# Two transformer blocks in one kernel: the normalised activations are placed at other byte offsets

## The reference

```
a = rmsnorm(h, norm1); proj = a @ w_in            # pool input, q/k/v of two kinds of attention, forget gates
h = h + concat(pool, forgetting attention, stick-breaking attention) @ w_out
h = h + (silu(n @ w_gate) * (n @ w_up)) @ w_down   # n = rmsnorm(h, norm2), inner width 2816
x = rmsnorm(h, final_norm)[:, 16:]
```

```
x = x + 0.5 * rmsnorm(swiglu(rmsnorm(x), w_ffn1_in, w_ffn1_out))
x = x + rmsnorm(mixer(rmsnorm(x)))                 # a gated convolution and a two-directional mLSTM
x = x + 0.5 * rmsnorm(swiglu(rmsnorm(x), w_ffn2_in, w_ffn2_out))
```

## Time and profile before

| | |
|---|---|
| median of 3 executions | 793.31 us (793.28 to 793.38) |
| the profiled execution | 793.85 us, its span 792.0 us |
| instructions | 12209 |
| TensorE busy, weight loads busy | 781.6 us (99%), 687.9 us |
| VectorE, ScalarE, GpSimd busy | 533.2, 429.3, 28.3 us |
| matmuls | 4710 |
| read from HBM | 139.69 MB, 178 GB/s over the span |

### The profile page before, as it was taken

How to read it: one execution, slowest core, us unless ns; L and a number is a source line. 1 busy time by engine, 2 the same in 40 slices (tenths; PEclk the granted TensorE clock), 3 DMA queues, 4 the chain that set the end, 5 groups by cost and what they waited for, 6 DMA issues and landing times.

```text
span 792.0 us, 12209 instructions
## 1 busy us (share of the span) xinstructions
PE 781.6 (99%) x4710; PEld 687.9 (87%) x4710; DVE 533.2 (67%) x628; ACT 429.3 (54%) x565; POOL 28.3 (4%) x35
## 2 busy tenths in 40 slices
PE   9999999999999999999999999999999999999997
PEld 8989988888888888888888887999988888888885
DVE  7866657766666667866666566766977766666665
ACT  6556657544544448744544447565557654454444
POOL 0000000000000000000000000002520000000000
PEclk9999999999999999999999999999999999999999
DMA  9633433645555553665545554452444664555521
GB/s 335 235 110 112 143 115 128 245 166 205 191 183 209 175 196 110 238 224 199 198 176 209 183 188 159 142 204 108 161 165 162 221 223 166 205 192 183 208 106 54
DMA packets 20797, 141.16 MB, mean 178 GB/s; under 512 B 2448, under 2 KB 2704, under 8 KB 4384
## 3 DMA queue, kind: packets, MB, share of 16 engines
q1 hardware_dynamic: 20192, 138.65, 48.8%
q0 software_dynamic: 576, 2.10, 0.8%
HBM read 139.69 MB, written 1.05 MB: 178 GB/s over the span
## 4 chain that ended last, share of the span: by engine, by line
PE 94%; ACT 2%; DVE 2%; issue 1%; DMA 1%; SPq 0%; DVEq 0%; ACTq 0%
PE ps L1478 93%; ACT whi L695 1%; PE ps L1484 1%; DMA raw<-wstream 1%; DVE x L1227 0%; ACT squared L710 0%; DVE xa L1034 0%; PE ps L1707 0%; DVE wlo L1023 0%; PE ps L1677 0%; PE ps L1926 0%; DVE xg L1222 0%; DVEq L272 0%; ACT L928 0%; PE ps L1709 0%
## 5 line engine op out<-in xcount | busy, mean ns | idle before, releaser
L1478 PE MATMUL ps<-xa,whi 128*128 128x512 f32 (+2 forms) x1744 | 377.4, 347 | 0.0
L1023 DVE TENSOR_TENSOR wlo<-raw,whi 128x2048 fp32r<-128x2048 f32 x128 | 293.6, 2295 | 82.2 <-ACT whi L695 82.2
L1478 PEld LDWEIGHTS ps<-xa,whi 128*128 128x128 f32 x1744 | 299.6, 188 | 41.4 <-issue 2.1
L695 ACT ACTIVATE whi<-raw 128x2048 fp32r<-128x2048 f32 x128 | 244.2, 1909 | 6.9 <-PE ps L1478 6.8
L1478 PE MATMUL ps<-xa,wlo 128*128 128x256 f32 (+1 forms) x1376 | 219.8, 278 | 0.0
L1478 PEld LDWEIGHTS ps<-xa,wlo 128*128 128x128 f32 x1376 | 187.9, 188 | 2.8
L1478 PE MATMUL ps<-wlo,hhi 128*128 128x512 f32 x240 | 93.5, 390 | 0.0
L1478 PE MATMUL ps<-whi,hlo 128*128 128x512 f32 x240 | 93.5, 390 | 0.0
L1478 PE MATMUL ps<-whi,hhi 128*128 128x512 f32 x240 | 93.5, 390 | 0.0
L889 ACT ACTIVATE hhi<-arena 128x512 fp32r<-128x512 f32 x30 | 19.0, 633 | 88.4 <-PE ps L1478 81.9
L875 ACT ACTIVATE arena<-ps 128x512 f32<-128x512 f32 x33 | 19.7, 597 | 85.5 <-PE ps L1478 85.4
(11 more groups left out here) (221 smaller groups left out, 531.6 us busy)
## 6 DMA issues: line engine op xcount, KB each, us to landing
raw<-wstream SPq DMA_DIRECT2D x128, 1024.0 KB, 4.8
gain_row<-rows_in POOLq DMA_DIRECT2D x4, 512.0 KB, 3.9
x<-x_in SPq DMA_DIRECT2D x2, 512.0 KB, 4.0
raw<-wstream SPq DMA_DIRECT2D x2, 512.0 KB, 5.8
out<-x SPq DMA_DIRECT2D x4, 256.0 KB, 2.1
xg<-const_in SPq DMA_DIRECT2D x1, 912.0 KB, 11.8
small<-small_in SPq DMA_DIRECT2D x1, 152.0 KB, 6.1
arena<-meta_in SPq DMA_DIRECT2D x1, 64.0 KB, 4.5
```

What stands on the lines that cost most here:

```text
L695: nc.scalar.activation(whi[slot][:], raw[slot][:], ACT.Copy).then_inc(hi_ready, 1)
L1023: nc.vector.tensor_tensor(wlo[slot][:], raw[slot][:], whi[slot][:].bitcast(F32), ALU.subtract).then_inc(lo_ready, 1)
L1478: return nc.tensor.matmul(o, lhsT, rhs, start=start, stop=stop, skip_group_check=True)
```

## The change

The start of the view `xn[k]` moves. In bytes from the beginning of `xa` it was 320 for all four. Now it is 128 in the first FFN, 256 in the second, 448 in the mixer and 384 in the third FFN. Which half of a tile is high and which is low stays as it is (`XN_HI`). No instruction, wait or transfer is added or removed.

```diff
--- before.py
+++ after.py
@@ -46,7 +46,7 @@
 GROUPS = FF // 256
 UNIT = 2048
 SLOTS = 3
-XN_AT = ((80, SEQ),) * 4
+XN_AT = ((32, SEQ), (64, SEQ), (112, SEQ), (96, SEQ))
 XN_HI = (0, 0, 0, 0)
 EPS = 1e-6
 NEG = -1e30
```

## The result

The changed kernel takes 800.59 us (800.46 to 801.46, 3 runs) against 793.31: 1.009 of the time of before, 95% interval 1.0076 to 1.0104. It is slower by 7.3 us, where I had forecast slower by 2.9 and a range to 799.5. The profiled execution has a span of 798.6 us against 792.0, at a full clock again.

The account below looks back on a forecast made before the run. TensorE, busy 781.6 of 792.0 us, was taken to bound the kernel. Low products +3.8, second FFN's 512-column products -0.9 and mixer 0 gave +2.9 us: 796.2 us from a median of 793.31, range 790.0 to 799.5.

Parts of the forecast that it names:

- What bounds the kernel: Whole kernel: TensorE sets the end, so any change in the distance between two matmuls' starts arrives one for one.
- The low products lose the clean pace: FFN loops: 256-column low products go from 113.4 ns to the slow pace, +3.8 us, 1.27 for each FFN.
- The 512-column products: FFNs: gate and up products gain only in the second FFN; worst case for all 1008 was +2.0 us.
- The second FFN like the down products: Second FFN at 256 bytes: its 512-column products reach the clean pace of products at distance zero, -0.9 us.
- The sum: Whole kernel: 3.8 - 0.9 + 0 = +2.9 us.
- The mixer unchanged: Mixer, from 320 to 448 bytes: taken as 0 us, since its token-major units already show both paces.
- The two paces: 256-column products: two steady paces at one distance, 113.4 (clean) and 117.8 ns (slow), chosen by what stood before the row.
- slower by more: Whole kernel: at a bad distance each product meets a collision that does not resolve, up to 801.6 us; chance 0.07.
- The rival that nothing changes: Whole kernel: nothing changes or parts cancel, within 0.2% (1.6 us) of 793.3 us; chance 0.30.

Follow-up runs that it names:

- e3: Kernel before with only the mixer's offset moved, from 320 to 448 bytes: 793.61 us, ratio 0.9996 (no measurable difference).
- e11: Kernel before, all offsets 320, with the mixer's product of each head's output with the sigmoid gate left out: 793.54 us.
- e12: Kernel before with the mixer at 448 bytes and its product with the sigmoid gate left out: 792.54 us.
- e1: Kernel before with offsets of 64, 192 and 448 bytes in the three FFNs and 448 in the mixer: 797.15 us.
- e5: Kernel before with the weight slots moved by 128 bytes and the activations by 256, through two unused tensors: 801.49 us.
- e7: Kernel before with the small products that spread the reciprocal root moved ahead of each FFN's first gate products: 793.84 us, ratio 1.0.
- e13: Kernel before with the edits of e3 and e7 together: 793.69 us, ratio 0.9994.

## Why the prediction was wrong

- **What bounds the kernel**: right in the FFNs. Nearly all of the difference is in the distance between starts of products there, with no wait added, and the clock stayed full. In the mixer it was not right that what TensorE gains arrives one for one: of 1.06 us 0.27 arrived (e3), and a wait of 0.5 us for VectorE's line 1389 came in, in the changed kernel too.
- **The low products lose the clean pace**: right in all three FFNs, the size too small. I took 117.8 ns; it was 118.8 at 128 and 384 bytes and 119.7 at 256. For 288 products in each FFN that is 1.6 us in one of the first kind and 1.8 in the second, where I had 1.27. In sum 4.9 us, for 3.8 forecast. The 119.7 lies above the 118.9 that I had taken as the worst.
- **The 512-column products**: this is the step that failed. I put their term at nothing in the first and third FFN, kept them at 229.4 ns there, and bounded their worst case by the longest duration among those at 320 bytes, 2 ns over the mean. At 128 and 384 they take 233.1 ns, outside that bound: 336 x 3.7 = 1.2 us in each of the two FFNs, 2.5 us in all. They do not settle there: the distance between starts goes back and forth between about 229 and 237 ns. The range of one row's durations at one distance is no bound for another distance.
- **The second FFN like the down products**: right. At a distance of 0 modulo 256 its 512-column products run at 226.9 ns where their operands' row has settled, -0.6 us with the slower entry of the up products (3.65 us for 16), for -0.9 forecast. The pattern of 256 bytes that I read from a query tile was confirmed by e1 and by the pair 128 and 384.
- **The sum**: 4.9 + 2.5 - 0.6 - 0.24 (mixer) = 6.6 us, of 7.03 between the stages. The rest, some 0.5 us, is left for the FFNs' first units and first groups, which I did not split further.
- **The mixer unchanged**: right within 0.24 us, for the wrong reason. Its column tiles did change, to 113.3 ns, and its second value unit lost its clean pace. Together that was 1.06 us gained up to the output units, and VectorE took most of it back (e3, e11, e12). That the sum came out near nothing is luck.
- **The two paces**: too simple. 256-column products are not either 113.4 or 117.8. At 128, 384 and 256 bytes their mean lies above both (118.8 and 119.7), at 336 and 352 it is 120.0, and at 368 it lies between (115.6).
- **The rival "slower by more"**, to which I gave 0.07: the time that came lies in it. Its mechanism, products that find no even pace at a bad distance, fits the 512-column products at 128 and 384, and the low products of the FFNs (118.8 and 119.7 ns). It does not fit the mixer, whose column tiles became faster.
- **The rival that nothing changes**: refuted. Modulo 256 bytes e5 moved only the weights, and the down products went from 227.1 to 233.3 ns with no wait on any semaphore. The Trainium skill (page "SBUF — State Buffer", section "Who interferes with whom") calls TensorE's two read ports independent. This case does not agree with what I drew from that, a distance worth 0 us; the measurement decides.

That two reads of one engine meet in the memory is the picture that fits, but it was only argued. Shown is that the distance of the two operands sets the pace, and that it repeats every 256 bytes in the three pairs tried. Open is why 64 is the best of the 13 distances, and what at a row's entry chooses its rhythm.

## What to carry to other kernels

When TensorE sets the end and runs back to back, measure the distance between starts in each row of equal products, not their mean durations. Where it is above the best such row, move one operand by 4 to 64 bytes and look again: here the same instructions took from 16.42 to 16.87 us a group, so up to 2.7%. Here each shape had its own best distances, and a gain arrives only where no other engine is close behind.

## What the runs showed that I had not expected

- Four bytes matter: 324 in place of 320 costs 0.45 us a group, the 512-column products going to 3.84 / 16 = 240 ns in the up unit.
- The best distance for products of 512 columns, 0, is the worst of the multiples of 64 for those of 256: 226.9 and 119.7 ns.
- The rhythm survives for whole stages: in the kernel before each of the 27 unbroken loop groups of the FFNs takes 16.42 us, and in the one after each takes 16.73 in the first and third FFN.
- Two unused tensors of 128 bytes, one ahead of the weights and one behind them (e5), cost 7.6 us, 1.0%, in a kernel in which nothing else changed.
- The same code at the same addresses ran a row of 32 products at 117.8 ns in e7 and at 113.4 in e13.
